# Two places in a beat of attention instead of three: scores and products together, transposes half a beat later

## The reference

```
first block    A (diff, 4 heads)   p0, p1 = softmax(q k + bias) of two halves;  o = (p0 - lam * p1) v, then an RMS norm
               B (8 heads)         a window of 128 keys back, with a sink in the softmax
               C (8 heads)         gated sum of three: compressed keys (31), selected keys (all), window keys (all)
second, twice  A (8 heads)         chunked, with a bias by relative position
               C (8 heads)         logits + (cq - ck), causal ("forgetting")
every branch   y = branch @ w_branch;  x += sum(sigmoid(gate) * y) @ w_out;  MLPs around it
```

## Time and profile before

| | us |
|---|---|
| median of three runs | 3692.1 |
| profiled execution | 3694.05 |
| its span, first to last instruction | 3692.2 |
| TensorE busy | 3460.3 |
| VectorE busy | 1424.1 |
| ScalarE busy | 758.1 |
| GpSimd busy | 2375.1 |

### The profile page before, as it was taken

One profiled execution on the slowest core, in us unless ns is written; L12 is line 12 of the kernel. 1 busy time (PEld: TensorE's weight loads), 2 busy tenths in 40 slices (PEclk: granted clock), 3 DMA queues, 4 the chain that ended last, 5 costly groups with the idle time before them and its releaser, 6 DMA issues.

```text
span 3692.2 us, 39941 instructions
## 1 busy us (share of the span) xinstructions
PE 3460.3 (94%) x15930; PEld 2704.8 (73%) x15930; DVE 1424.1 (39%) x2582; ACT 758.1 (21%) x1480; POOL 2375.1 (64%) x1238
## 2 busy tenths in 40 slices
PE   7876999999999998978999999999999889999999
PEld 6553666788878887756777888788876557787887
DVE  5755664243353224564433111232245654322111
ACT  2534332111121001243221100110012432211000
POOL 6413444877768776543668777777774436687775
PEclk9978999999999999999999999999999999999999
DMA  3212122354435443211233223254431112232222
GB/s 134 64 57 69 58 64 72 100 194 165 165 114 205 174 157 114 75 57 50 87 96 100 92 97 97 91 195 166 164 125 64 63 48 86 77 108 86 97 97 74
DMA packets 104185, 387.93 MB, mean 105 GB/s; under 512 B 11824, under 2 KB 12080, under 8 KB 97856
## 3 DMA queue, kind: packets, MB, share of 16 engines
q1 hardware_dynamic: 87984, 292.76, 24.1%
q10 hardware_dynamic: 16016, 92.62, 6.5%
HBM read 383.20 MB, written 2.13 MB: 104 GB/s over the span
## 4 chain that ended last, share of the span: by engine, by line
PE 86%; DVE 9%; ACT 3%; issue 2%; DMA 0%; ACTq 0%; DVEq 0%
PE psum L1035 27%; PE psum L1036 26%; PE psum L1037 26%; PE psum L1103 2%; PE psum L1145 2%; PE psum L1120 2%; DVE rs_t L1430 1%; PE psum L1090 1%; DVE s_sb L1470 1%; ACT s_sb L1256 1%; DVE s_sb L1507 1%; DVE neg_max L1475 1%; ACT sq_t L1230 0%; PE psum L1082 0%; DVE res L1584 0%
## 5 line engine op out<-in xcount | busy, mean ns | idle before, releaser
L1003 POOL TENSOR_TENSOR w_hi<-raw,ones 128x1024 fp32r<-128x1024 f32 (+3 forms) x591 | 1043.5, 1766 | 1142.5 <-PE psum L1037 1133.1
L1006 POOL TENSOR_TENSOR w_lo<-raw,w_hi 128x1024 fp32r<-128x1024 f32 (+3 forms) x591 | 1315.9, 2227 | 46.3
L1035 PE MATMUL psum<-h_hi,w_hi 128*128 128x512 f32 (+1 forms) x2744 | 1123.1, 409 | 52.2 <-DVE r L1445 25.5
L1036 PE MATMUL psum<-h_lo,w_hi 128*128 128x512 f32 (+1 forms) x2744 | 1084.8, 395 | 0.0
L1037 PE MATMUL psum<-h_hi,w_lo 128*128 128x512 f32 (+1 forms) x2744 | 1084.7, 395 | 0.0
L1035 PEld LDWEIGHTS psum<-h_hi,w_hi 128*128 128x128 f32 (+1 forms) x2744 | 523.3, 191 | 209.6 <-issue 47.3
L1037 PEld LDWEIGHTS psum<-h_hi,w_lo 128*128 128x128 f32 (+1 forms) x2744 | 522.8, 191 | 115.6
L1036 PEld LDWEIGHTS psum<-h_lo,w_hi 128*128 128x128 f32 (+1 forms) x2744 | 524.1, 191 | 106.9 <-issue 5.5
L1035 PE MATMUL psum<-a_hi,w_hi 128*128 128x512 f32 x960 | 375.3, 391 | 12.6 <-DVE x L1704 12.6
L1696 DVE TENSOR_TENSOR psum<-g_sb,psum 128x512 f32<-128x512 f32 x120 | 83.5, 696 | 785.6 <-PE psum L1037 699.2
L1036 PE MATMUL psum<-a_lo,w_hi 128*128 128x512 f32 x960 | 374.8, 390 | 0.0
(11 more groups left out here) (189 smaller groups left out, 3256.0 us busy)
## 6 DMA issues: line engine op xcount, KB each, us to landing
raw<-weights_dram SPq DMA_DIRECT2D x489, 512.0 KB, 3.4
ada_t<-ada_dram ACTq DMA_DIRECT2D x48, 1536.0 KB, 7.1
raw<-weights_dram SPq DMA_DIRECT2D x72, 256.0 KB, 2.6
raw<-weights_dram SPq DMA_DIRECT2D x32, 384.0 KB, 3.0
bias_t<-biases_dram ACTq DMA_DIRECT2D x36, 256.0 KB, 2.8
bias_t<-cum_dram ACTq DMA_DIRECT2D x16, 256.0 KB, 3.7
out_dram<-x SPq DMA_DIRECT2D x8, 256.0 KB, 2.0
raw<-weights_dram SPq DMA_DIRECT2D x4, 408.0 KB, 3.1
```

What stands on the lines that cost most here:

```text
L1003: nc.gpsimd.tensor_tensor(high, piece, ones[:, 0:1].to_broadcast([P, n]), ALU.mult)\
L1006: nc.gpsimd.tensor_tensor(w_lo[:, p % NR, 0:n], piece, high.bitcast(F32), ALU.subtract)\
L1035: mm(dst, lh, rh, start=first, stop=False)
L1036: mm(dst, lh, rl, start=False, stop=False)
```

## The change

The step `copy` is put right behind `turn` of the same duo. A beat now has three functions: scores of duo j+2 followed at once by products of duo j, with weight 2w; transposes and copy of duo j+1, with weight w; scaling of duo j+2, with weight w. The output step, the start of a root and the count of the masks stay inside `products` and move with it.

```diff
@@ def turns(j), in attend
             for b in T_BANKS[:len(u.t_before)]:
                 HELD[b] = ("pt_copied", u.n)
             put("turn", u)
+            put("copy", u)
 
     def products(j):
@@
             u.need_v = READY[V_AT[kind]]
             put("pv", u)
-        if 0 <= j + 1 < n:
-            put("copy", duos[j + 1])
         if 0 <= j and duos[j].last:
@@
     for j in range(-2, n):
         w = 1 + max([d.blocks for d in duos[max(0, j):j + 3]])
-        out += [(lambda j=j: scores(j), w), (lambda j=j: turns(j), w), (lambda j=j: products(j), w),
-                (lambda j=j: scale(j), w)]
+        out += [(lambda j=j: (scores(j), products(j)), 2 * w), (lambda j=j: turns(j), w), (lambda j=j: scale(j), w)]
```

## The result

The changed kernel took 3705.81 us, the median of eight runs between 3694.57 and 3709.36; the kernel before took 3692.62 beside it (eight runs, 3688.64 to 3697.33). The ratio is 1.003 with a 95% interval of 1.0019 to 1.004, which is 7 to 15 us; the medians differ by 13 us: slower. The forecast was 3674 and faster; the time lies outside its range too. The profiled execution took 3706.05 us, its span 3704.3, 12.1 longer than the span before.

The account below looks back on a forecast made before the run. TensorE's throughput was taken as the bound (busy 94%). Terms -8 - 12.8 + 7.6 + 2.4 - 2 - 2 - 3.4 = -18.2 us took 3694.05 to 3675.9; the run median lies 1.95 lower, so 3674, range 3660 to 3684.

Parts of the forecast that it names:

- part 5: Side effects: output steps done sooner -2 us, root sums -2 us, earlier masks 0, att_a 0; the clock -3.4 us.
- att_a changed by more than 3 us: Sign against the forecast: it would mean that the root's earlier start matters, which was put at nothing.
- Part 2: TensorE in att_c and the two att_a2: scores and products adjoining save 0.2 us of switching each, 74 places, -8 us.
- Part 3: Transposes come later, so their waits for scaled probabilities shrink: att_c -7, att_b -3, both att_a2 -2.8; sum -12.8 us.
- Part 4: Products come earlier and wait for ScalarE's copy: +7.6 us in att_b and att_c, +2.4 at att_a2's forget steps.
- The clock (-3.4): Half-clock stretches of TensorE behind one long wait each in att_c and att_b may go: 1.7 us each, -3.4.
- Rival (b): Slower: products wait for copies coming 1 us later, 34 us of new waits; +11.6, so 3704 us; chance 0.14.
- (a): Nothing to measure: VectorE and ScalarE's softmax chain sets the pace, switches cost as before; 3689 us; chance 0.23.
- (c): More gain: two thirds of the transposes' waits go (-30 us), adjacencies give -15; 3646 us; chance 0.13.
- T's waits under 20 us: Sign for the forecast: the transposes' waits for VectorE in att_b and att_c fall from 30.3 us to under 20.
- Copy waits of 5 to 12 in att_b and att_c: Sign for the forecast: new TensorE waits for ScalarE's copy in these two stages, 5 to 12 us in all.
- att_c2 was to stay within 2 us of 172: Sign for the forecast: the length of stage att_c2 stays within 2 us of its 172.

Follow-up runs that it names:

- experiment 1: The changed kernel with the start of the root put back behind the transposes and copy, in att_a alone; 3681.8 us.
- experiment 2: The changed kernel with only the sum of att_a's early root, and the square root and reciprocals behind it, one stretch of projection work later; 3683.4 us.
- experiment 3: The changed kernel with every output step, root start and mask count back behind the transposes, in all stages; 3674.1 us.
- experiment 7: The changed kernel with output steps and root starts back behind the transposes in all stages, the mask count left early; 3673.7 us.
- experiment 4: The kernel before with only the products with the values moved, right behind the scores; transposes, copy and output step at their old places; 3685.0 us.
- experiment 9: The changed kernel with output steps, root starts and mask count back behind the transposes, except the output step early in att_c2; 3675.1 us.
- masks late: The changed kernel with the mask count behind the transposes everywhere and the root start late in att_a alone, output steps early elsewhere; 3678.3 us.
- mixed by stage: The changed kernel with outputs behind the transposes, but att_a2 in the order of the kernel before and the output step early in att_c2; 3676.5 us.

## Why the prediction was wrong

**The step that failed is part 5**, "side effects": it priced the outputs at -2 us, the root sums at -2, and att_a at 0, because there "S waits for P, which the moves don't touch". The moves did touch it. The start of a root moved half a beat ahead, and its square root and reciprocals, queued behind stretches of projection work, moved with it from behind P to in front of P on VectorE and from behind the copy to right behind the exponentials on ScalarE. Measured: +18.5 us in att_a (experiments 1, 2 and 3; 11.9 of it waits), +6.6 and +6.7 in att_a2 (3 and 7; some 4.9 of each waits), 31.7 in all by the medians and 25 to 32 by the ratios, against the -4 of the forecast. The forecast followed the waits that end at an output step and saw that they would get shorter, which they did (VectorE's at the output step in att_b from 9.1 us to 4.9); it did not list what is queued behind such a step on ScalarE and VectorE and who needs that. It did name the sign by which this would be seen: att_a changed by more than 3 us.

**Part 2 (switches, -8) was right in size for each.** In att_c S and V adjoin 46 times in the changed kernel and twice in the one before; 44 times 0.21 us, worked out below, is 9.2, and TensorE's busy time there fell from 235.01 us to 226.16 for the same number of groups and at the same clock of 0.97, by 8.8. In the kernel before, V and S of one kind stand alone between projections in att_c:

```profile
395.74 0.40 PE L1037 MATMUL psum<-h_hi,w_lo 128*128 128x512 f32 x1
396.07 1.09 PE L1145 MATMUL psum<-pt_sb,v_bc 128*64 128x128 f32 x16
397.09 0.50 PE L1035 MATMUL psum<-h_hi,w_hi 128*128 128x512 f32 x1
...
398.35 0.40 PE L1037 MATMUL psum<-h_hi,w_lo 128*128 128x512 f32 x1
398.68 0.70 PE L1103 MATMUL psum<-k,r 64*128 64x256 f32 x4
399.31 0.50 PE L1035 MATMUL psum<-h_hi,w_hi 128*128 128x512 f32 x1
```

The changed kernel has them together:

```profile
404.90 0.39 PE L1035 MATMUL psum<-br_a,w_lo 128*128 128x512 f32 x1
405.22 0.70 PE L1101 MATMUL psum<-k,r 64*128 64x256 f32 x4
405.85 1.09 PE L1143 MATMUL psum<-pt_sb,v_bc 128*64 128x128 f32 x16
406.88 0.50 PE L1033 MATMUL psum<-h_hi,w_hi 128*128 128x512 f32 x1
```

From the start of the last projection product to the start of the next, alone they take 1.35 and 0.96 us, together 1.98. The difference is 0.33; 0.23 of it is the pitch of a projection product, which the separate ones count once more, and behind each the first projection product takes 0.11 more than its pitch (0.34), once instead of twice. So an adjacency saves 0.33 - 0.23 + 0.11 = 0.21 us; the forecast had 0.2. Going from S to V shows nothing: 0.63 us from one start to the other, as from S to a projection. The Trainium skill, "TensorEngine Tiling (Array Packing)", Key Properties, says that a change of the tiling mode drains the TensorE. By that rule the change from 64-row to 64-column tiles would cost as much as the others, one drain in four would go and 0.1 us be saved; the rows show two of four gone, so here the measurement decides against that reading of it. In att_c2, where the two mask products lie between S and V, the saving is 0.08 us (by the same reckoning 2.29 for 4 scores of 384, masks and 16 products together, against 1.13 and 1.24 apart); the forecast counted none there. In att_c V early alone took 7.8 us off the busy time (experiment 4). The 8 us are thus reached in att_c alone; what the 28 places in the two att_a2 gave is not separated from their clock.

**Part 3 (T later, -12.8) was right for T's own waits, and too careful there.** T's waits fell by 17.3 us in att_b and att_c, and those of T in att_a2 went altogether (7.5 each, the largest of them into V's new wait). But less came of them. In att_b S waited 5.9 us more for the maxima, a wait that the forecast did not have, and TensorE's idle time fell by only 5.2 us there and by 4.6 in att_c. T late alone shortened att_c by 11.4 us, 5.3 of them idle time.

**Part 4 (V waits for the copy, +7.6 and +2.4) was about right.** Measured: 3.3 in att_b, 3.7 in att_c, 7.2 and 6.9 in the two att_a2, of which 6.51 at the first layer's forget step, where T no longer waits its 6.13. Not foreseen was V's wait of 3.3 and 1.1 us for VectorE's output step, which frees V's bank; in att_b it is as large as that for the copy.

```profile
1577.04 1.98 PE L1143 MATMUL psum<-pt_sb,v 128*64 128x128 f32 x16 [6.51 <-ACT pt_sb L1269]
```

**The clock (-3.4) gave nothing in the changed kernel.** Att_b's granted clock was 0.79 instead of 0.84 and att_c's 0.97 as before; it was 0.99 in experiment 3. Att_b's busy time was 2.0 us longer for three groups more.

**The rest of the sum.** Without part 5's outputs and root sums the forecast's terms add to -14.2 us; the kernel with only these moves in it gained 18.5 by the medians and 14 by its ratio. That it came to 3674.1, the forecast's own number, is partly chance: a term that was too small (the switches), one that was never there (the -4 of part 5), one that it lacked (S's waits in att_b) and a higher clock in att_a, worth some 3 us, all went into the measured gain.

**The rivals.** Rival (b) gave 3704 us, 2 off the time, and its mechanism is not what happened: it needed 34 us of new copy waits beside those of the forget steps, and there are 8.1 (21.0 in all, 12.9 at the forget steps). Experiment 3 has the same moves of V and T and is 18.5 us faster than before. (a) and (c) fell. No rival held a step that moves along with V and stands in another engine's loop; it should have been the rival of the other side.

**The signs named in advance.** T's waits under 20 us: 13.0. Copy waits of 5 to 12 in att_b and att_c: 7.0. One of about 7 us in each att_a2: 6.51. S to V under 0.9 us: 0.63. Att_c shorter by over 5 us: 13.3. Wrong: att_c2 was to stay within 2 us of 172 and is 168.0; of the 3.5 us, 1.0 is the gate's wait (1.2 us before, 0.2 now, see experiment 9) and about 2 the eight or nine groups that now run behind the stage. And att_a moved by 15.5.

## What to carry to other kernels

When a step is moved, follow everything it starts, on every engine, and ask for each of these what then stands behind it; a wait that gets shorter says nothing about the instructions behind the one that waits. In a loop over engines (here scores, maxima, exponentials, scaling, scores) a foreign instruction in front of the loop's own can cost TensorE time, however idle its engine is on average (ScalarE 43% and VectorE 60% busy in att_a). And take a change apart on the chip before it is judged: two of its moves together gained 14 to 21 us, and the third, which came along with V, lost 25 to 32. And put idle time and clock apart before a stage's length is read: what "masks late" seemed to give back in att_a2, and what "mixed by stage" seemed to lose in att_a, was clock.

## What the runs showed of the hardware

**VectorE beside GpSimd.** The pair of scalings of 128x512 from SBUF to SBUF takes 0.88 us, and 3.87 us where GpSimd's two splits (1.89 and 2.40 us) ran at the same time, as the rows of experiment 7 show: VectorE was free again 0.3 us after the second split ended. A pooling copy of 128x4, 0.17 us in the kernel before, took 2.25 in the changed kernel (at 1655.37 us) beside another split of 2.92. The Trainium skill, "SBUF — State Buffer", section "Who interferes with whom", says that the two share a port pair, and that an instruction of VectorE in a two-port mode waits until GpSimd's is over; the trace agrees. It makes VectorE's times depend on where GpSimd happens to be: a start 2.0 us later cost 3.0 more.

**The clock of a stage differs without a change in its order or its idle time.** The granted clock of att_a was 0.89 in the kernel mixed by stage and 0.94 or 0.95 in the eight other experiments, and the first of these idled no more than experiment 3 (25.2 us against 26.1); it was worth 5.6 us of busy time. Each kernel has one profiled execution, so whether this belongs to the kernel or to the execution is not shown; the mean clock of one kernel, that of before, went from 0.970 to 0.975 over its executions. A stage's length alone doesn't tell an effect of that size from the clock's; the busy time of the same instructions does.
